# Expert weights of a mixture-of-experts decoder step: first-matrix transfers of two units against four

## What is computed

```python
logits = (t @ w_router + b_router)
top_v, top_e = lax.top_k(logits, TOP_K)              # 4 of 32
gates = jax.nn.softmax(top_v, axis=-1)
def expert_block(args):
    xb, e = args                                     # the rows of expert e
    hh = xb @ w1[e] + b1[e]                          # 1024 -> 2048
    glu, lin = jnp.split(hh, 2, axis=-1)
    glu = jnp.minimum(glu, SWIGLU_LIMIT)
    lin = jnp.clip(lin, -SWIGLU_LIMIT, SWIGLU_LIMIT)
    act = glu * jax.nn.sigmoid(SWIGLU_ALPHA * glu) * (lin + 1.0)
    return act @ w2[e] + b2[e]                       # 1024 -> 1024
```

## Time and profile before

| | us |
|---|---|
| median of 3 runs | 1245.54 |
| lowest and highest | 1244.42, 1245.88 |
| the profiled execution, device time | 1242.38 |
| its span in the trace | 1240.7 |

### The profile page before, as it was taken

The page is one execution under the profiler, slowest core; times in us unless marked ns, Lnnn a source line. Parts: engine busy times, 40 slices in busy tenths (PEclk is TensorE's granted clock), DMA queues, the critical chain, the costliest instruction groups (busy, mean ns, idle before and its releaser), DMA issues.

```text
span 1240.7 us, 16218 instructions
## 1 busy us (share of the span) xinstructions
PE 1160.5 (94%) x6549; PEld 577.8 (47%) x6549; DVE 387.7 (31%) x729; ACT 232.3 (19%) x405; POOL 62.9 (5%) x102
## 2 busy tenths in 40 slices
PE   7999999997999999999998989898989898989996
PEld 5778899887434344343333333332323232323332
DVE  3555768377221222212121213131121212121214
ACT  3342244144101111010111011110101110111012
POOL 5302001123000000000000000000000000000000
PEclk9999999997999999999999999999999999999999
DMA  9833399996899999999999999999999999999994
GB/s 312 258 129 102 113 327 340 360 346 263 327 428 428 427 428 429 428 428 429 428 428 429 429 427 428 429 428 428 429 428 428 429 429 428 428 429 428 428 428 169
DMA packets 79748, 466.52 MB, mean 376 GB/s; under 512 B 4384, under 2 KB 51008, under 8 KB 54912
## 3 DMA queue, kind: packets, MB, share of 16 engines
q1 hardware_dynamic: 72816, 455.36, 89.7%
q0 software_dynamic: 1504, 6.13, 1.5%
q10 hardware_dynamic: 5392, 4.54, 1.2%
HBM read 460.32 MB, written 5.70 MB: 376 GB/s over the span
## 4 chain that ended last, share of the span: by engine, by line
PE 65%; DMA 30%; DVE 2%; ACT 1%; issue 1%; SPq 0%; ACTq 0%; DVEq 0%
DMA ring<-w 30%; PE bank L1739 21%; PE bank L1774 12%; PE bank L1356 9%; PE bank L1526 5%; PE bank L1714 5%; PE bank L1694 4%; PE bank L1514 2%; PE bank L1758 1%; ACT rest L801 1%; PE bank L1695 1%; PE bank L1586 1%; DMA ring<-w_in 1%; PE bank L1611 1%; PE bank L1557 1%; PE bank L1570 1%
## 5 line engine op out<-in xcount | busy, mean ns | idle before, releaser
L1739 PE MATMUL bank<-ring,rest 128*64 128x512 f32 x2048 | 457.8, 595 | 38.1 <-DMA ring<-w 31.7
L1739 PEld LDWEIGHTS bank<-ring,rest 128*64 128x64 f32 x2048 | 142.7, 136 | 333.0 <-issue 256.0
L1774 PE MATMUL bank<-ring,rest 128*64 128x512 f32 x1024 | 226.8, 595 | 17.0 <-ACT rest L801 17.0
L1281 DVE TENSOR_SCALAR rest<-bank 128x512 f32<-128x512 f32 x32 | 22.1, 692 | 486.9 <-PE bank L1739 486.9
L1774 PEld LDWEIGHTS bank<-ring,rest 128*64 128x64 f32 x1024 | 71.3, 137 | 151.2 <-issue 134.9
L1260 DVE TENSOR_TENSOR rest<-rest,bank 128x512 f32<-128x512 f32 (+1 forms) x102 | 66.9, 680 | 227.8 <-PE bank L1714 227.7
L1356 PE MATMUL bank<-rest,ring 128*128 128x288 f32 (+1 forms) x512 | 125.4, 405 | 8.5 <-DMA ring<-w_in 8.5
L797 ACT ACTIVATE rest<-rest 128x512 f32<-128x512 f32 x32 | 20.2, 630 | 523.4 <-DVE rest L1281 523.4
L1356 PEld LDWEIGHTS bank<-rest,ring 128*128 128x128 f32 x512 | 97.6, 192 | 33.9 <-DMA ring<-w_in 8.5
L1714 PE MATMUL bank<-rest 128*128 128x512 f32 (+1 forms) x204 | 98.4, 611 | 1.3 <-ACT rest L809 1.3
L809 ACT COPY rest<-bank 64x512 f32<-64x512 f32 x64 | 37.1, 580 | 225.2 <-PE bank L1774 224.5
(11 more groups left out here) (292 smaller groups left out, 712.8 us busy)
## 6 DMA issues: line engine op xcount, KB each, us to landing
ring<-w SPq DMA_DIRECT2D x192, 2048.0 KB, 33.5
ring<-w_in SPq DMA_DIRECT2D x12, 1024.0 KB, 12.0
ring<-k_t SPq DMA_DIRECT2D x8, 1024.0 KB, 12.3
ring<-v_c SPq DMA_DIRECT2D x8, 1024.0 KB, 7.2
ring<-w_xk SPq DMA_DIRECT2D x4, 1024.0 KB, 4.9
ring<-w_xv SPq DMA_DIRECT2D x4, 1024.0 KB, 4.9
ring<-w_out SPq DMA_DIRECT2D x4, 1024.0 KB, 7.6
ring<-w_xq SPq DMA_DIRECT2D x4, 1024.0 KB, 12.6
```

The source lines that it names most:

```text
L1739: last = t.matmul(out, slots[:, k, :], w[:, col], start=False, stop=(k == KT - 1))
L1774: last = t.matmul(ps[2][CAP * ds:CAP * ds + CAP, :], actT[:, at:at + CAP], w[:, b, 512 * ds:512 * ds + 512], start=(a == 0 and b == 0), st ...
```

## The change

Three things, in one edit.

1. `w1` comes in transfers of four units into four neighbouring slots; partition p gets four neighbouring rows, 32 KB in one piece. `w2` stays at two units and 16 KB. The table `TRANSFERS` lists what a turn loads, `(first unit, number)`. A transfer of n units waits for `units_used` of j + n - 16, and PE waits once for four units of `w1`.
2. The ring's first expert slot moves from 6 to 8 (`EXP_AT`), so that groups of four begin at slots 0, 4, 8 and 12. The first ring is now filled by five transfers (4, 4, 2, 2 and 4 units), behind the uses of `U_VC + 4`, `U_XO + 1`, `U_XO + 2`, `U_XO + 3` and `U_XO + 3`.
3. The columns of each half of `hx` are stored in the order 0, 4, 8, ..., 1, 5, 9, ... so that the gather reads 128 neighbouring columns. For that, ACT's and DVE's instructions that make `hx_hi` and `htmp` read `y` (and the accumulation bank) with a step of four elements, and write in sequence.

```diff
+EXP_AT = 8
+RUN = 4
+TRANSFERS = [(EXP_UNITS * b + q, n) for b in range(BODY) for q, n in ((0, RUN), (RUN, RUN), (8, 2), (10, 2))]
...
+        def by_run(v):
+            return v.rearrange("t (p r) -> t r p", r=RUN)
+
+        def runs(v):
+            return v.rearrange("t (r p) -> t r p", r=RUN)
...
-        def load_expert_units(eng, e, j):
+        def load_expert_units(eng, e, j, n):
 
-            s, q = (j + PRE) % SLOTS, j % EXP_UNITS
+            s, q = (j + EXP_AT) % SLOTS, j % EXP_UNITS
             e = e + j // EXP_UNITS
-            both = cells(s * SLOT, (s + 2) * SLOT)
+            units = cells(s * SLOT, (s + n) * SLOT)
             if q < W1_UNITS:
-                src = w1[e, q * P:(q + 2) * P, :].rearrange("(p r) c -> p (r c)", r=2)
+                src = w1[e, q * P:(q + n) * P, :].rearrange("(p r) c -> p (r c)", r=n)
...
-                for j in range(first, BODY * EXP_UNITS, 2):
-                    sp.wait_ge(units_used, g * (BODY * EXP_UNITS) + j + 1 - SLOTS + 1)
-                    load_expert_units(sp, i * BODY, j)
-            for u, j in ((U_KC + 4, 6), (U_VC + 3, 2), (U_VC + 4, 4), (U_VC + 7, 0), (U_XO + 1, 8),
-                         (U_XO + 2, 10), (U_XO + 3, 12), (U_XO + 3, 14)):
+                for j, n in TRANSFERS:
+                    if j >= first:
+                        sp.wait_ge(units_used, g * (BODY * EXP_UNITS) + j + n - SLOTS)
+                        load_expert_units(sp, i * BODY, j, n)
+            for (j, n), u in zip(TRANSFERS, (U_VC + 4, U_XO + 1, U_XO + 2, U_XO + 3, U_XO + 3)):
                 wait_unit_used(sp, u)
-                load_expert_units(sp, 0, j)
+                load_expert_units(sp, 0, j, n)
...
-                a.activation(hx_hi[tt][0:R, 0:512], y[0:R, tt, 0:512], ACT.Copy, scale=yrs[0:R, tt:tt + 1]).then_inc(h_hi, 1)
+                a.activation(runs(hx_hi[tt][0:R, 0:512]), by_run(y[0:R, tt, 0:512]), ACT.Copy, scale=yrs[0:R, tt:tt + 1]).then_inc(h_hi, 1)
...
-                v.scalar_tensor_tensor(htmp[tt][0:R, q], y[0:R, tt, q], yrs[0:R, tt:tt + 1], hx_hi[tt][0:R, q],
+                v.scalar_tensor_tensor(runs(htmp[tt][0:R, q]), by_run(y[0:R, tt, q]), yrs[0:R, tt:tt + 1], runs(hx_hi[tt][0:R, q]),
...
-                    cols_d = slice(256 * (d // 2) + d % 2, 256 * (d // 2) + 256, 2)
+                    cols_d = slice(P * d, P * d + P)
...
-                        if u % 2 == 0:
-                            pe.wait_ge(ring_in[s], (BODY * EXP_UNITS // SLOTS * g + (fills(s) + fill + 1)) * 16)
+                        if any(first == unit for first, n in TRANSFERS):
+                            pe.wait_ge(ring_in[s], (transfers_into(s, BODY * EXP_UNITS) * g
+                                                    + (fills(s) + transfers_into(s, unit) + 1)) * 16)
```

## The result

The changed kernel takes 1249.79 us (median of 6 runs, 1246.67 to 1250.51) where the kernel before takes 1245.14 us (6 runs, 1243.90 to 1246.01): a ratio of 1.0038, 95% interval 1.0028 to 1.0049. It is slower by 4.7 us; 1251.1 had been forecast, within 1246 to 1259. The profiled execution took 1247.93 us with a span of 1246.2 us, 5.5 us above the 1240.7 us of before. The sum had said 5.6, but two of its terms were off and a third was missing, in opposite directions.

The account below looks back on a forecast made before the run. The transfer stream was taken as the bound from its gapless start, then PE's work behind the last `w1` data. 3.4 + 3.4 + 1.8 - 3.0 = +5.6 us on 1245.54 gave 1251.1 us, range 1246 to 1259.

Parts of the forecast that it names:

- The first refill waits for four units: Start of the expert stream: first refill held from 314.39 to 317.82 us, never given back; cost 3.4 us.
- The gap that the prediction had at 339 us: Early stream: old and new kernel have one gap each, at 336 and 339 us, of the same size.
- a sign of being wrong: Forecast wrong if the pair period changes over 0.5 us or a gap opens in the stream between 340 and 600 us.
- Four units behind the last landing: End of the last expert's `w1`: PE has four units to do, 7.02 us in place of 3.65; cost 3.4 us.
- Stepped reads: Before the first gather: DVE's six `rest_part` instructions 0.3 us longer each; cost 1.8 us, between 0 and 4.
- Longer rows: `w1` stream: half the rows disappear at 6.1 ns each; gain 3.0 us, from nothing to 4 to 5.
- The two-point line: Row time from 4 KB rows (416 GB/s, 157.5 ns) and 16 KB rows (428.5 GB/s, 611.8 ns): 6.1 ns fixed.
- Moved early transfers and the gather: Ring filling before the experts and PE's weight loads: later early transfers cost nothing, the gather's gain counted as nothing.
- A: `w1` stream: fixed time per transfer or row halved, 17.9 us gained against 8.6 of costs, 1236 us; chance 0.09.
- B: No measurable change: stepped reads cost nothing, longer rows give 4.7 us; +2.1, 1247.6 us; chance 0.14.
- C: `w1` stream: 32 KB rows stream worse, 1% less rate; +14.6 us, 1260 us; chance 0.08.
- D: Before the first gather: stepped reads cost 4 us, not 1.8; 1253.3 us, counted within the forecast's 0.69.

Follow-up runs that it names:

- experiment 2: Changed kernel with four-unit transfers cut into 16 KB rows, layout, reads and gather as before the change: 1249.41 us, ratio 1.0051 to the kernel before.
- experiment 3: Kernel before with one number changed, the first refill waits until PE has used four units, not two: 1244.89 us, ratio 1.0005.
- experiment 6: Changed kernel with units 4 to 7 in two transfers of two: 1247.94 us, ratio 1.0035; with plain reads as well: 1244.77 us, 1.0008.
- experiment 7: First-turn four-unit `w1` refills split in twos: on the changed kernel 1246.34 us; on that with plain reads and units 4 to 7 in twos 1242.10 us.
- experiment 4: Kernel before, transfers still two units, but PE waits for four `w1` units at units 0 and 4: 1248.37 us, ratio 1.0032.
- experiment 1: Changed kernel with `hx` columns in natural order, so plain reads, and PE's gather picking every fourth column: 1247.02 us, ratio 1.0024.

## Why the prediction was right, point by point

*What bounds the kernel.* Right: the stream from its first refill to the last `w1` landing, then PE. Each experiment that moved one of the three intervals moved the end by it.

*The first refill waits for four units: 3.4 us forecast, 2.9 measured* (experiment 2 against before, with the same rows). It went out at 319.67 us, 6.9 behind the first product, as said. The gap that the prediction had at 339 us is there, 1.85 us later with the first product, so it is not a new gap of the kind that the prediction names as a sign of being wrong. Its size is roughly the old one: 262 GB/s at 340 to 345 us are 1.9 us missing, where the kernel before misses 1.5 at 335 to 345. The prediction overlooked a second, smaller gap in the kernel before: 374 GB/s at 325 to 330 us, 0.6 us missing, where experiment 2's kernel has 426. Its closing would account for the 0.5 us between 3.4 and 2.9; no experiment tests it by itself. That the first refill is the place of the loss was too narrow: with it alone delayed 1.9 us are lost (experiment 3), with it alone brought back nothing is gained (experiment 6). It takes every four-unit transfer of the ramp (experiment 7).

*Four units behind the last landing: 3.4 us forecast, 3.4 measured* (experiment 4; the profiled execution of the changed kernel has a further 1.7 us from the clock). That fall of the clock was not in the sum. The step that failed is the sentence that PE takes 7.02 us for four units: it took the duration from the early stretch where PE never pauses and used it behind a pause of 2.6 us. The pause itself could have been worked out, since four units land 9.8 us apart and PE needs 7.1 for them.

*Stepped reads: 1.8 us forecast, 1.85 measured,* with parts that don't fit as well. DVE's instructions cost 0.38 us more each and not 0.3, so the last of its instructions for the third part ended 2.2 us later; the first product of the gather's second half came at 309.90 after 307.68, also 2.2 later, but the gather then ran sooner at the upper clock (0.51 us for its first six products in place of 0.82) and gave 0.4 back. ACT's three reads from on-chip memory cost 0.49 us more each, at the upper end, the three from the banks nothing; together 1.5 us, which left ACT just ahead of DVE. By the Trainium skill (Vector Engine (DVE) Microarchitecture Reference, section 5.2), 1.73 in place of 1.054 ns a column for one source that hops at every element, 512 columns would cost 0.35 us more, an estimate. The measured 0.38 us at a step of four is nearer to it than to the 0.3 us from the short rows.

*Longer rows: 3.0 us forecast, 4.4 measured* (experiment 2). The mechanism was right, the size was not: 8.9 ns a row in place of 6.1. The two-point line rested on one window of 5 us with 4 KB rows at 416 GB/s. For 8.9 ns it would have to read 411, while windows of 2 us beside it read 394 to 424, so such a short window can't carry the working. The stated upper end, 4 to 5 us, held it, but not for the reason given, the completions: fewer transfers at equal rows give nothing (experiment 2). The period of a pair fell to 58.45 us, not 58.53.

*Moved early transfers and the gather: nothing,* as forecast. The refills went out in time, and experiment 1 finds 0.1 us at most for the gather's columns.

*Sum:* 1.85 + 2.9 + 3.4 + 1.7 - 4.4 = 5.5 us, the difference of the spans. That 5.6 had been forecast is in part luck: the 1.7 us of the clock, which it left out, cancel against the 1.4 us of the rate and the 0.5 us of the refill. One of its own signs failed by this: behind the last wait PE has a piece of 8.78 us and not of 7.0. The medians differ by 4.7 us, less than the two profiled executions, which lie 2.8 us (before) and 1.9 us (changed) below their medians. In how many executions the clock falls in the last expert isn't known.

*The rivals.* A (a rate that pays for it all): the rate rose, but by 4.4 us and not 17.9; 8.6 would have paid for the costs as forecast. B falls with the measured interval (3.5 to 6.1 us against its 2.1), C with the rate, D with the reads' 1.85 us against its 4. What none of them said: 2.9, 3.4 and 1.85 us belong to four-unit transfers and stepped reads at a few places, and the gain in rate isn't bound to them. The kernel of 1242.10 us shows it: in the middle units 0 to 3 of each expert keep rows of 32 KB, units 4 to 7 come in rows of 16 KB, the start of the stream is as fine as before, and the reads are plain. It keeps half of the gain in rate.

## What to carry to other kernels

A larger transfer into a ring has three prices that its rate doesn't show: the stream stalls in front of the first large refill that it catches up with, the last one leaves more work behind its landing, and the pause in front of it can cost PE its clock. Here each counted once, since in the middle PE was ahead of the stream, while the gain in rate counted in every expert. So small transfers belong at the ramp and the end and long rows in the middle. The kernel of 1242.10 us does this for half of the rows of `w1`; one with four units everywhere but at the ramp and in the last expert, and plain reads, was not run. If a layout needs a stepped read, put the step where it is free; here that was PE's weight load (at most 0.1 us) and reads from the accumulation banks, and not DVE's or ACT's reads of fp32 from on-chip memory.

## What the runs showed of the hardware

- With `w1` (two thirds of the bytes) in rows of 32 KB and `w2` in rows of 16 KB the stream runs at 430 to 431 GB/s; with 16 KB rows throughout, at 428 to 429. The difference is 8.9 ns for each row that an engine is spared. Four units in one transfer instead of two change nothing at equal rows (58.75 and 58.73 us a pair).
- A read of 512 fp32 elements with a step of four from on-chip memory costs DVE 1.12 in place of 0.74 us with one such operand, and ACT 1.21 in place of 0.71 us. From an accumulation bank ACT loses nothing: 0.66 us with the step, 0.67 without.
- PE's granted clock was at its upper level (2.4 GHz) before each pause of 2.2 to 2.6 us and fell to the lower one (1.2 GHz) in five of twelve cases just behind the restart, for a loss of 1.7 us each (seven of twelve in experiment 2, six of eleven in experiment 4). With the pause filled with products it never fell there, and neither in the kernel before, whose pauses in front of `w1` products there are 1.3 us at most. What decides between the cases stays open.
